# A transformer block pair on one core: the split inputs and all buffers behind them moved up by 128 bytes

## The reference, cut to what matters

```python
h = rmsnorm(x, norm_mix_g)
u = h @ w_in                                  # 2048 x 12288
c_g, b_g, xa, za, q, fl, iv, og, ga, gb = jnp.split(u, split_idx, axis=-1)
ya = b_g * causal_dwconv3(c_g * xa, conv_w) * jax.nn.silu(za)
...                                           # recurrence over 8 heads -> yb
m = jax.nn.sigmoid(ga) * (ya @ w_a_out) + jax.nn.sigmoid(gb) * (yb @ w_b_out)
x = x + m @ w_o
gate = jax.nn.sigmoid(rmsnorm(x, ple_norm_g) @ w_ple_gate)
x = x + gate * (p @ w_ple_proj)
```

## Time and profile before

| | |
|---|---|
| median of three runs | 2564.58 us (2564.48 to 2564.61) |
| span of the profiled execution | 2563.3 us |
| TensorE busy (matmuls) | 2548.6 us, 99% |
| TensorE weight loads | 2106.7 us, 82% |
| VectorE busy | 1342.8 us, 52% |
| ScalarE busy | 941.9 us, 37% |
| GpSimd busy | 79.1 us, 3% |
| granted TensorE clock, mean | 0.998 |
| DMA | 309.29 MB, mean 121 GB/s |

### The profile page before, as it was taken

The page is one execution under the profiler, slowest core; times in us unless marked ns, Lnnn a source line. Parts: engine busy times, 40 slices in busy tenths (PEclk is TensorE's granted clock), DMA queues, the critical chain, the costliest instruction groups (busy, mean ns, idle before and its releaser), DMA issues.

```text
span 2563.3 us, 31667 instructions
## 1 busy us (share of the span) xinstructions
PE 2548.6 (99%) x13058; PEld 2106.7 (82%) x13058; DVE 1342.8 (52%) x2151; ACT 941.9 (37%) x1326; POOL 79.1 (3%) x64
## 2 busy tenths in 40 slices
PE   9999999999999999999999999999999999999998
PEld 8887888887888888888888888888888888888888
DVE  7556734457534555655543363584355545554425
ACT  6543324333323222322232353443344344443423
POOL 0000000000000000000001103200000000000000
PEclk9999999999999999999999999999999999999999
DMA  5322223322234666666443222235312222222424
GB/s 193 110 83 79 87 91 99 91 77 80 92 93 142 220 215 210 217 213 217 144 161 107 99 91 101 96 91 182 98 59 82 84 82 82 74 83 83 166 97 156
DMA packets 159984, 309.29 MB, mean 121 GB/s; under 512 B 11040, under 2 KB 15392, under 8 KB 158816
## 3 DMA queue, kind: packets, MB, share of 16 engines
q1 hardware_dynamic: 159040, 305.70, 36.9%
q0 software_dynamic: 224, 1.15, 0.1%
q10 hardware_dynamic: 576, 0.42, 0.1%
HBM read 298.84 MB, written 8.39 MB: 120 GB/s over the span
## 4 chain that ended last, share of the span: by engine, by line
PE 98%; DVE 2%; ACT 0%; issue 0%; DVEq 0%
PE bank L341 91%; PE bank L1291 1%; PE bank L1292 1%; PE bank L1293 1%; PE bank L810 1%; PE bank L755 1%; PE bank L1457 1%; PE bank L763 0%; PE bank L1631 0%; DVE CGB L2135 0%; DVE EE L460 0%; DVE EE L462 0%; DVE XX L465 0%; DVE XX L455 0%; ACT XX L445 0%; ACT XX L447 0%
## 5 line engine op out<-in xcount | busy, mean ns | idle before, releaser
L341 PE MATMUL bank<-XH,WH 128*128 128x512 f32 (+1 forms) x2880 | 1110.1, 387 | 1.3 <-DVE TMP L1003 0.5
L341 PE MATMUL bank<-XH,WL 128*128 128x512 f32 (+1 forms) x2880 | 1101.9, 385 | 0.0
L341 PE MATMUL bank<-XL,WH 128*128 128x512 f32 (+1 forms) x2880 | 1101.9, 385 | 0.0
L391 DVE TENSOR_TENSOR WL<-RAW,WH 128x1024 fp32r<-128x1024 f32 x443 | 546.2, 1234 | 794.9 <-ACT WH L368 794.0
L368 ACT CAST WH<-RAW 128x1024 fp32r<-128x1024 f32 x443 | 464.0, 1049 | 1061.1 <-PE bank L341 1057.5
L341 PEld LDWEIGHTS bank<-XH,WH 128*128 128x128 f32 x2880 | 540.8, 188 | 111.3 <-DVE TMP L1003 1.3
L341 PEld LDWEIGHTS bank<-XH,WL 128*128 128x128 f32 x2880 | 540.7, 188 | 108.8 <-DVE WL L391 0.2
L341 PEld LDWEIGHTS bank<-XL,WH 128*128 128x128 f32 x2880 | 541.0, 188 | 106.4 <-issue 0.5
L341 PE MATMUL bank<-WH,XH 128*128 128x512 f32 x384 | 150.1, 391 | 0.0
L341 PE MATMUL bank<-WH,XL 128*128 128x512 f32 x384 | 149.5, 389 | 0.0
L341 PE MATMUL bank<-WL,XH 128*128 128x512 f32 x384 | 149.5, 389 | 0.0
(11 more groups left out here) (307 smaller groups left out, 1796.4 us busy)
## 6 DMA issues: line engine op xcount, KB each, us to landing
RAW<-in_w_in SPq DMA_DIRECT2D x303, 512.0 KB, 3.6
AST<-in_w_ada SPq DMA_DIRECT2D x192, 256.0 KB, 4.1
RAW<-in_w_out SPq DMA_DIRECT2D x40, 512.0 KB, 3.4
RAW<-in_w_o SPq DMA_DIRECT2D x32, 512.0 KB, 3.6
RAW<-in_w_gate SPq DMA_DIRECT2D x32, 512.0 KB, 3.4
RAW<-in_w_a SPq DMA_DIRECT2D x16, 512.0 KB, 4.2
RAW<-in_w_b SPq DMA_DIRECT2D x16, 512.0 KB, 4.2
XT<-in_xT SPq DMA_DIRECT2D x4, 1024.0 KB, 6.8
```

The source lines that it names most:

```text
L341: ins = nc.tensor.matmul(bank[b][:, cols], l, r[:, cols], start=first, stop=final)
L391: nc.vector.tensor_tensor(WL[:, m % NSPL], RAW[:, m % NRAW], WH[:, m % NSPL].bitcast(F32), ALU.subtract).then_inc(lo.sem, lo.step(m))
```

## The change

The offsets of XH, XL and C0 grow by 128 bytes. W0 is computed from C0, and with it every buffer behind. Two buffers that lie inside XL's room by number, ONE0 and SC, get the same 128 bytes. RAW, WH and WL keep their places. No instruction changes but for the addresses.

```diff
     RAW = sb("RAW", [NRAW, 2, 512], F32, 0)
     WH = sb("WH", [NSPL, 2, 512], F32R, 16384)
     WL = sb("WL", [NSPL, 2, 512], F32R, 28672)
-    XH = sb("XH", [16, 512], F32R, 40960)
-    XL = sb("XL", [16, 512], F32R, 73728)
-    C0 = 106496
+    XH = sb("XH", [16, 512], F32R, 41088)
+    XL = sb("XL", [16, 512], F32R, 73856)
+    C0 = 106624
     ONES_R = sb("ONES_R", [128], F32R, C0)
     ONES = ONES_R[:, :].bitcast(F32)
-    ONE0 = sb("ONE0", [128], F32, 73728 + 10 * 2048)
+    ONE0 = sb("ONE0", [128], F32, 73856 + 10 * 2048)
...
-    SC = sb("SC", [5, 512], F32, 73728 + 11 * 2048)
+    SC = sb("SC", [5, 512], F32, 73856 + 11 * 2048)
```

## The result

The changed kernel takes 2619.41 us (median of four runs, 2618.91 to 2620.81) against 2564.60 us before (four runs). The ratio is 1.0213, with a 95% interval of 1.0201 to 1.0226: it is slower by 54.8 us. The likeliest case of the prediction was no change, 2564.6 us; what came is its rival on the slow side, to which the prediction gave a chance of 0.31. The stated range of 2536 to 2628 us holds the result only because that rival's price was its upper edge.

A forecast was written before the change was run, and what follows sets the result against it. TensorE's dense matmul step of 226.6 ns was taken to bound the kernel. All terms were 0, so the span stayed 2563.3 us; 1.3 us up to the median of runs gave 2564.6 us, range 2536 to 2628 us.

The forecast's parts named there:

- slower rival: Dense matmuls: 128 bytes keep TensorE's two reads out of their rest state; 232.5 ns steps, +63 us, 2628 us; chance 0.31.
- What bounds the kernel: TensorE, busy 2548.6 of 2563.3 us; dense matmuls stepping at 226.6 ns make 2374 us, 93% of the span.
- Term (1), the dense pairs: Streamed operand against weights loaded beside it, shifted by 128 bytes: bounded from -116 to +107 us, taken as 0.
- faster rival: At 128 bytes the dense reads get out of each other's way: 2536 us half-way, 2448 in full; chance 0.23.
- Terms (2) to (4): Stretches disturbed by transposes and attention scores (3 us at most), ScalarE and VectorE on shifted buffers, transfers: each taken as 0.
- The signs named beforehand: In 100 us, 443 dense records if unchanged, 432 if slower, 465 if fully faster; both operand orders follow if distance counts.

## Why the prediction was wrong in its first choice

**What bounds the kernel** held. TensorE's step is the time; every kernel here follows it, and the idle time of the other engines only grew (1061.1 to 1105.8 us before the casts of L368).

**Term (1), the dense pairs, is the step that failed.** I bounded it from -116 to +107 us and took 0, on the ground that the recovery to 226.6 ns looked like a rest state of the two reads and that a pattern repeating each 128 bytes was the least that explains the 64-byte rows. The recovery is real, but only at distance 0. At 128 bytes no rest state near 226.6 ns was seen: the steps go on between 0.23 and 0.24 us to the end, 232.4 ns in the mean. The two kernels that moved by 128 and by 256 bytes show that the pattern repeats each 256 bytes and not each 128, the case that the text named as fitting every row as well. The rows had the distances 0, 32 (EH) and 64 (QH) and nothing between 64 and 192, and a weak reason was preferred to an open question. The reading that "a distance of 64 bytes costs some 10 ns" was too high as well: with all dense pairs at 64 bytes the step is 228.7 ns, 2.1 more, and 233 at 192. The 237 ns at QH were those of three matmuls that kick the step, not of a steady run.

**The slower rival's size.** It said +5.9 ns on 10,656 matmuls, +63 us. The step rose by 5.8 ns. Measured are 54.8 us, for two reasons that can be counted. The 384 half-wide matmuls did not slow down (119.9 to 118.7 ns), which takes off 384 x 5.9 ns = 2.3 us. And 226.6 ns is the rest state before, not its mean: with the disturbed stretches, which stood near 232 ns already, the 512-column steps of the whole trace average 227.05 ns before and 232.55 after, so the rise is 5.5 ns on 10,272, 56.5 us. TensorE's idle time fell by 1.8 us besides (from 2563.3 - 2548.6 = 14.7 to 2617.6 - 2604.7 = 12.9 us). Added up over records, the nine large dense groups grew by 56.4 us (for example 1110.1 to 1125.0 and 150.1 to 152.2 us), the span by 54.3.

**The faster rival** is excluded for this layout: of the eight distances none has a mean step below 226.6 ns. Its argument, that two reads that begin at one byte at one moment would meet, pointed the wrong way, for that is the best placement. The page "TensorE: Matmul & The Clock Gate" of the Trainium skill (section "Step-by-step: what each phase is for") says that the load of the next weights takes nothing from the running matmul; 100 us with 443 records at one distance and 428 at another speak against it for these operands. Its section "Back-to-back issue gap" gives 518 cycles, near 216 ns, as the gap of an isolated matmul of 512 columns, and about 131 ns for a stream of weight loads and matmuls. The 11 ns a step that the first figure would leave to win no placement here gave, and the second one is far below every mean step of these kernels, 226.6 to 234.6 ns.

**Terms (2) to (4)** were right to be small: the split of the weights kept 1049 and 1235 ns, and in the kernel with all buffers 128 bytes up every shifted access of ScalarE, VectorE and the transfers was there at no cost (ratio 0.9998).

**The signs named beforehand** came as written for the slower rival: 432 records in 900 to 1000 us, and both orders of operands affected. That the number is that near is in part luck: the 232.5 ns were the average of eight steps behind a group of transposes, and nothing in the trace before said that a distance of 128 bytes would give the same. One sign is not clean: TR, VR and PL keep their distances, and yet the records of PL,TR and PR,VR went from 389 to 391 ns in the mean and those of PR,TR, which often come first behind a dense matmul, from 389 to 394. The prediction would have read this as the absolute address counting. The kernel with all buffers up by 128 excludes that, as there all three are at 389 again; what is left is that the disturbance runs on from the dense matmuls into these.

**What stays open.** That TensorE's two reads meet somewhere is the reading that fits; no run shows where or how, only that their distance decides most of it. The order of the eight distances (64 far better than 32 and 96) has no explanation here. A matmul can be long when the weights already in use are the ones off the distance, and, in one rhythm of the kernel with XL moved, when none of its own operands is off. That a load's reads reach beyond its record would fit the first, and no run tests it. That a long step always lengthens the next is contradicted: in 1400 to 1480 us of that kernel the record of 395 ns is followed by one of 388.

## What to carry to other kernels

Where TensorE is busy without a gap, read its step from a count of records in a stretch, not the mean duration. If it is longer than in another stretch of like matmuls, or if single steps differ, compare the addresses of the stationary and the moving operands modulo 256 bytes. In this kernel, to have all dense fp32r operands at one byte modulo 256 was the best of eight placements, and a stray 32 to 224 bytes between weights and input cost 1 to 2.7% with no instruction changed.

## What the runs showed of the hardware that was not expected

- TensorE's step of a 512-column fp32r matmul depends on the distance of its two operands in a partition modulo 256 bytes: 226.6 ns at 0, 228.7 at 64, 232.4 to 234.6 at the other six multiples of 32 below 256.
- The sign counts: +64 and -64 differ by 4 ns, and they change places when the moving and the stationary operand do.
- At distance 0 the step repeats to its rounding (226 or 227 ns) and is found again mostly within ten matmuls after a disturbance. At 128 it does not settle in a span of 2617.6 us. At 96 it keeps a pattern of three: 231, 232 and 237 ns all through 1000 to 1100 us.
- With XL alone off by 128 bytes the same addresses gave two lasting rhythms: 344 records in 80 us in one stretch, 351 in another.
- 256-column matmuls took no harm: 118.7 against 119.9 ns.
